# Neighbourhood attention with tokens ordered by grid columns: blocks of 64 queries over 128 keys

## The reference

```python
col = jnp.arange(GRID_W)                       # GRID_W = 64
col_start = jnp.clip(col - NA_COLS // 2, 0, GRID_W - NA_COLS)      # NA_COLS = 16
col_mask = (col[None, :] >= col_start[:, None]) & (col[None, :] < col_start[:, None] + NA_COLS)
...
sc = jnp.einsum('bhqd,bhrkd->bhqrk', qi, kr).astype(jnp.float32)
sc = sc + jnp.transpose(bias, (0, 2, 1, 3))[None]
sc = jnp.where(col_mask[:, None, :], sc, NEG_INF)
p = jax.nn.softmax(sc.reshape(b, N_HEADS, GRID_W, kh * GRID_W), axis=-1).reshape(sc.shape)
return jnp.einsum('bhqrk,bhrkd->bhqd', p.astype(vr.dtype), vr)
```

## Time and profile before

| | us |
|---|---|
| median of 3 runs | 1767.66 (1767.57 to 1767.67) |
| the profiled execution, its own time | 1768.03 |
| its span in the trace | 1766.1 |
| PE busy | 1757.5 |
| DVE busy | 1232.5 |
| ACT busy | 994.0 |
| POOL busy | 97.8 |

### The profile page before, as it was taken

One profiled execution on the slowest core, in us unless ns is written; L12 is line 12 of the kernel. 1 busy time (PEld: TensorE's weight loads), 2 busy tenths in 40 slices (PEclk: granted clock), 3 DMA queues, 4 the chain that ended last, 5 costly groups with the idle time before them and its releaser, 6 DMA issues.

```text
span 1766.1 us, 25241 instructions
## 1 busy us (share of the span) xinstructions
PE 1757.5 (100%) x9960; PEld 1503.2 (85%) x9960; DVE 1232.5 (70%) x1897; ACT 994.0 (56%) x1580; POOL 97.8 (6%) x179
## 2 busy tenths in 40 slices
PE   8999999999999999999999999999999999999999
PEld 7878888888888888888888888888888888888887
DVE  5877774668776677567755887776487648778763
ACT  6666553555555655456545666554565446656551
POOL 0000000511110000000001110000000001100000
PEclk9999999999999999999999999999999999999999
DMA  9335565453343455545563344555365534336552
GB/s 354 133 145 189 191 227 191 178 189 144 144 155 144 168 191 203 214 150 187 190 215 132 132 167 162 200 189 214 138 218 191 214 122 168 144 143 215 191 212 75
DMA packets 45080, 314.72 MB, mean 178 GB/s; under 512 B 5008, under 2 KB 5520, under 8 KB 7968
## 3 DMA queue, kind: packets, MB, share of 16 engines
q1 hardware_dynamic: 44640, 312.54, 48.8%
q10 hardware_dynamic: 288, 0.52, 0.1%
q0 software_dynamic: 32, 0.03, 0.0%
HBM read 312.03 MB, written 1.05 MB: 177 GB/s over the span
## 4 chain that ended last, share of the span: by engine, by line
PE 99%; DMA 0%; DVE 0%; ACT 0%; SPq 0%; issue 0%
PE P L404 96%; PE P L699 1%; PE P L411 1%; DMA raw<-w_all 0%; ACT xx L1239 0%; PE P L1117 0%; PE P L1037 0%; PE P L605 0%; DVE xx L1790 0%; PE P L983 0%; DVE xs L1810 0%; PE P L1060 0%; PE P L931 0%; ACT wh L1217 0%; PE P L921 0%
## 5 line engine op out<-in xcount | busy, mean ns | idle before, releaser
L1755 DVE TENSOR_TENSOR wl<-raw,wh 128x2048 fp32r<-128x2048 f32 x287 | 656.9, 2295 | 190.4 <-ACT wh L1211 171.3
L1211 ACT ACTIVATE wh<-raw 128x2048 fp32r<-128x2048 f32 x291 | 551.8, 1900 | 194.5 <-PE P L404 170.4
L404 PE MATMUL P<-xx,wh 128*128 128x512 f32 (+2 forms) x2800 | 652.1, 385 | 0.0
L404 PEld LDWEIGHTS P<-xx,wh 128*128 128x128 f32 (+1 forms) x2800 | 503.0, 188 | 100.1 <-issue 4.3
L404 PEld LDWEIGHTS P<-xx,wl 128*128 128x128 f32 x2688 | 344.4, 191 | 12.4
L404 PE MATMUL P<-xx,wl 128*128 128x256 f32 x2688 | 350.7, 283 | 0.0
L1340 ACT ACTIVATE ft<-P 128x256 f32<-128x256 f32 x240 | 90.3, 383 | 230.7 <-PE P L404 230.7
L404 PE MATMUL P<-wh,fhh 128*128 128x512 f32 x528 | 206.2, 390 | 0.0
L404 PE MATMUL P<-wh,fhl 128*128 128x512 f32 x528 | 205.5, 389 | 0.0
L404 PE MATMUL P<-wl,fhh 128*128 128x512 f32 x528 | 205.5, 389 | 0.0
L1916 DVE TENSOR_TENSOR fg<-P,ft 128x256 f32<-128x256 f32 x240 | 101.8, 424 | 121.7 <-ACT ft L1340 116.5
(11 more groups left out here) (323 smaller groups left out, 1485.5 us busy)
## 6 DMA issues: line engine op xcount, KB each, us to landing
raw<-w_all SPq DMA_DIRECT2D x289, 1024.0 KB, 4.8
nB<-rpb SPq DMA_DIRECT2D x4, 768.0 KB, 8.8
raw<-w_all SPq DMA_DIRECT2D x2, 512.0 KB, 7.3
fgb<-post SPq DMA_DIRECT2D x2, 512.0 KB, 5.5
out<-xs SPq DMA_DIRECT2D x4, 256.0 KB, 2.0
C<-cst SPq DMA_DIRECT2D x1, 769.0 KB, 7.9
xs<-x_in ACTq DMA_DIRECT2D x2, 256.0 KB, 3.9
xs<-x_in SPq DMA_DIRECT2D x1, 512.0 KB, 7.4
```

What stands on the lines that cost most here:

```text
L404: return t_.on.matmul(o, l, r, start=start, stop=stop, skip_group_check=True)
L1211: a.on.activation(o, i, ACT.Copy).then_inc(*hi.up((m,)))
L1755: v.on.tensor_tensor(o, i, h.bitcast(F32), ALU.subtract).then_inc(*lo.up(m))
```

## The change

The tokens of the attention step are ordered by grid column, number = 4 * column + row, while the rest of the kernel keeps the old order. A block of 64 queries (16 columns) then needs at most 32 columns, which are 128 neighbouring keys. Keys are kept at their number modulo 128, so that a tile of scores is 128 queries by 128 places.

- x is loaded in the new order into `nx` (the buffer `ntm`), and a second time in the old order into `xs`, after piece 10, for the residual sum.
- `scores_na` makes four blocks of 64 queries. `SEGMENTS` lists for each the pieces of keys (first key, place, width), six in all, and each is one matmul a head.
- Bias, maximum, exponential and scaling work on two times 128 columns a head instead of two times 256. The bias is 2 MB instead of 3 MB.
- Two transposes a head instead of four.
- `nV` has four parts: the values of the 128 keys of each block. ACT writes parts 0 and 3, and POOL builds parts 1 and 2 from them in twelve copies of 512 columns, six for each half of the heads. `values_na` makes one sum over 128 keys for each of four blocks of 64 queries.
- The output copies read PSUM in the order of columns and write in the old order (`natural`, `columns`).

```diff
+SEGMENTS = [[(0, 0, 128)], [(32, 32, 96), (128, 0, 32)], [(128, 0, 96), (96, 96, 32)], [(128, 0, 128)]]
...
+        def placed(t, d):
+
+            return x_in[0, :, d].rearrange("(r c) d -> c r d", r=4)[32 * t:32 * t + 32, :, :]
+
+        def natural(ap):
+            return ap.rearrange("p (r c) -> p r c", r=4)
+
+        def columns(ap):
+            return ap.rearrange("p (c r) -> p r c", r=4)
...
-            q.on.dma_start(xs[:, 1, :], x_in[0, toks(1), :]).then_inc(*s_x[1][0].up(0))
+            q.on.dma_start(nx[:, 1, :], placed(1, slice(0, D))).then_inc(*s_x[1][0].up(0))
...
+                if m == RAW + 7:
+                    q.on.dma_start(xs[:, :, :], x_in[0].rearrange("(t p) d -> p t d", t=2)).then_inc(*s_res.up(0))
...
-                for t in range(2):
-                    for h in range(2):
-                        q = AN["nq"][64 * h:64 * h + 64, p % 4, :]
-                        k = mul(P[2 + h][:, t * S:(t + 1) * S], q[:, toks(t)], q[:, S:2 * S], True, True)
+                for b in range(4):
+                    o = 64 * (b % 2)
+                    for key, at, w in SEGMENTS[b]:
+                        for h in range(2):
+                            q = AN["nq"][64 * h:64 * h + 64, p % 4, :]
+                            at_ = b // 2 * 128 + at
+                            k = mul(P[2 + h][o:o + 64, at_:at_ + w], q[:, 64 * b:64 * b + 64], q[:, S + key:S + key + w],
+                                    True, True)
...
-                t_.wait_ge(*aa.of("V", 0, 3))
-                for y in range(2):
+                t_.wait_ge(*aa.of("V", 0, p // 4))
+                t_.wait_ge(*aa.of("V", 0, 2 + p // 4))
+                t_.wait_ge(*ga.of("V", p // 4, 5))
+                for y in range(4):
                     for h in range(2):
                         t_.wait_ge(*aa.of("c", 0, p, h))
-                        k = mul(P[b][64 * h:64 * h + 64, 0:S], AN["nV"][:, y, (2 * p + h) * 64:(2 * p + h) * 64 + 64],
-                                NTA[h][:, y * S:(y + 1) * S], y == 0, y == 1)
+                        k = mul(P[b][64 * h:64 * h + 64, 64 * y:64 * y + 64],
+                                AN["nV"][:, y, (2 * p + h) * 64:(2 * p + h) * 64 + 64], NTA[h][:, 64 * y:64 * y + 64], True, True)
...
-                probs(0, p, NPA, (4, 5) if p < 7 else (2, 3), (0, 2, 1, 3))
+                probs(0, p, NPA, (4, 5) if p < 7 else (2, 3), (0, 1))
...
-                a.on.activation(AN["noh"][:, p, :], P[obank(p)][:, 0:S], ACT.Copy).then_inc(*ax.up(("oh", 0, p)))
+                a.on.activation(natural(AN["noh"][:, p, :]), columns(P[obank(p)][:, 0:S]), ACT.Copy).then_inc(*ax.up(("oh", 0, p)))
...
-                both_scores(0, p, NPA, AN["nsmA"], ((0, 256), (256, 256)), bias, 1.0)
+                both_scores(0, p, NPA, AN["nsmA"], ((0, 128), (128, 128)), bias, 1.0)
...
+                if s == 0:
+                    v.wait_ge(*s_res.of(0))
...
+            for hf in range(2):
+                g.wait_ge(*aa.of("V", 0, hf))
+                g.wait_ge(*aa.of("V", 0, 2 + hf))
+                if hf:
+                    g.wait_ge(*ga.of("V", 0, 5))
+                V_ = AN["nV"][:, :, halfs(hf)]
+                for i, (y, p0, p1, src) in enumerate(((1, 0, 32, 3), (1, 32, 64, 0), (1, 64, 128, 0), (2, 0, 64, 3), (2, 64, 96, 3),
+                                                      (2, 96, 128, 0))):
+                    if i:
+                        g.wait_ge(*ga.of("V", hf, i - 1))
+                    g.on.tensor_copy(V_[p0:p1, y, :], V_[p0:p1, src, :]).then_inc(*ga.up(("V", hf, i)))
```

More of the change, by code:

```diff
@@ L410, in turn @@
                 for j in range(4):
-                    k = t_.on.transpose(P[b][:, toks(j)], xs[:, t, (4 * q + j) * 128:(4 * q + j + 1) * 128], ident)
+                    k = t_.on.transpose(P[b][:, toks(j)], (xs if s else nx)[:, t, (4 * q + j) * 128:(4 * q + j + 1) * 128], ident)
                 k.then_inc(*tx.up(("turn", s, t, q)))
@@ L1243, in squares @@
                 a.wait_ge(*(s_x[t][h * (1 - t)].of(0) if s == 0 else vx.of("x", s - 1, h, t)))
-                a.on.activation(SQJ[s][:, t, halfs(h)], xs[:, t, halfs(h)], ACT.Square, bias=0.0, scale=1.0,
+                a.on.activation(SQJ[s][:, t, halfs(h)], (xs if s else nx)[:, t, halfs(h)], ACT.Square, bias=0.0, scale=1.0,
                                 accum_out=ss[:, 2 * h + t:2 * h + t + 1]).then_inc(*ax.up(("sq", s, h, t)))
@@ L1428, in probs_na @@
             def probs_na(p):
-                both_probs(0, p, NTA, (4, 5) if p < 7 else (2, 3))
+                both_probs(0, p, NTA, (4, 5) if p < 7 else (2, 3), 256)
             def exps_na(p):
-                exps(0, p, NPA, AN["nsmA"], ((0, 256), (256, 256)), 1.0)
+                exps(0, p, NPA, AN["nsmA"], ((0, 128), (128, 128)), 1.0)
             def probs_dil(n):
@@ L1460, in na @@
                 for i in range(4):
-                    a.on.activation(AN["nV"][:, i // 2, halfs(i % 2)], P[2 + i][:, :], ACT.Identity, bias=0.0,
+                    a.on.activation(AN["nV"][:, i // 2 * 3, halfs(i % 2)], P[2 + i][:, :], ACT.Identity, bias=0.0,
                                     scale=rr_[:, i // 2:i // 2 + 1]).then_inc(*aa.up(("V", 0, i)))
@@ L2017, in bias @@
                 def bias(h, z):
-                    at = (2 * p + h) * 384 + 128 - 128 * z
-                    return AN["nB"][:, at:at + 256]
-                both_scores(0, p, NPA, AN["nsmA"], ((0, 256), (256, 256)), bias, 1.0)
+                    at = (2 * p + h) * 256 + 128 * z
+                    return AN["nB"][:, at:at + 128]
+                both_scores(0, p, NPA, AN["nsmA"], ((0, 128), (128, 128)), bias, 1.0)
             def shares_na(p):
-                shares(0, p, NPA, AN["nsmA"], ((0, 256), (256, 256)))
+                shares(0, p, NPA, AN["nsmA"], ((0, 128), (128, 128)))
             def scores_dil(n):
@@ L2035, in out_na @@
                 v.wait_ge(*ax.of("oh", 0, p))
-                v.on.tensor_tensor(AN["nol"][:, p, :], P[obank(p)][:, 0:S], AN["noh"][:, p, :].bitcast(F32),
-                                   ALU.subtract).then_inc(*vx.up(("ol", 0, p)))
+                v.on.tensor_tensor(natural(AN["nol"][:, p, :]), columns(P[obank(p)][:, 0:S]),
+                                   natural(AN["noh"][:, p, :].bitcast(F32)), ALU.subtract).then_inc(*vx.up(("ol", 0, p)))
             def out_dil(f):
@@ L2669, in packed @@
             put(name, l, np.tile(inputs[name][l], (128, 1)))
-    rpb = np.full((2, 64, NH, 6, 64), NEG, np.float32)
-    for i in range(2):
-        for q in range(64):
-            a = min(max(q - 8, 0), 48)
-            b = a + 16
-            rpb[i, q, :, :, a:b] = inputs["na_rpb"][0][:, 5 - i:11 - i, a - q + 15:b - q + 15]
-    rpb = rpb.reshape(128, NH * 384)
+    rpb = np.full((128, NH, 2, 128), NEG, np.float32)
+    for n in range(256):
+        q, i = divmod(n, 4)
+        a = min(max(q - 8, 0), 48)
+        for k in range(4 * a, 4 * a + 64):
+            rpb[n % 128, :, n // 128, k % 128] = inputs["na_rpb"][0][:, k % 4 - i + 7, k // 4 - q + 15]
+    rpb = rpb.reshape(128, NH * 256)
     post = np.stack([inputs["norm_mix_post"][0], inputs["norm_ffn_post"][0], inputs["norm_mix_post"][1],
```

14 lines of the change are left out of this document (8 added, 6 removed).

## The result

| | before | changed |
|---|---|---|
| median, us | 1767.66 (1767.57 to 1768.0, 4 runs) | 1757.05 (1756.9 to 1757.1, 4 runs) |
| the profiled execution, its own time | 1768.03 | 1757.08 |
| its span | 1766.1 | 1755.3 |

The ratio is 0.9939, with a 95% interval from 0.9922 to 0.9957: the changed kernel is 10.6 us faster, where 9.0 were forecast: 1757.05 us lies under the 1757.8 to 1760.2 that the prediction gave to its own case A. The whole interval lies beyond the 0.2% that a measurement tells from no change.

The account below looks back on a forecast made before the run. TensorE was taken to bound the kernel. Transposes 3.5, sums of values 3.2 and scores 2.4 us gave 9.1, called 9.0: from 1768.03 to 1759.0, or 1758.7 us as a median; its own range was 1757.8 to 1760.2.

Parts of the forecast that it names:

- case A: The prediction's own case, all terms summed: 1758.7 us, range 1757.8 to 1760.2, chance 0.60.
- What bounds: TensorE bounds the attention section, so a microsecond of its work removed there is a microsecond off the end.
- Transposes, 3.5 us: TensorE's attention transposes: four fewer a pair at 0.11 us each, 3.5 us saved over eight pairs.
- Sums of values, 3.2 us: TensorE's sums of values: eight matmuls of 64 columns replace four of 256, 0.61 us instead of 1.01, saving 3.2 us.
- Scores, 2.4 us: TensorE's attention scores: twelve small matmuls started in program order, a group of 0.75 us instead of 1.07, saving 2.4 us.
- Rival B: Scores: array halves run freely and 32-column passes are cheap, saving 3.8 us; time 1757.3 us, chance 0.15.
- The start, 0: Program start: the read of x by grid column was counted as nothing, at most 0.5 us of lateness.
- What must stay hidden: Attention period: DVE at 7.4 us and ACT at 6.0 fit in 7.6; POOL's copies and DMA stay hidden too.
- The lateness at pair 1's scores: TensorE asks DVE earlier at pair 1's scores: about 0.3 us wait without gain from halved widths, none with; counted nothing.
- rival D: Every attention period: TensorE asks DVE too early and waits 0.3 to 0.6 us; time about 1762.5, chance 0.05.
- Rival E: Pair 0's sum of values waits for slow POOL copies, making the kernel slower: 1774.4 us, chance 0.03.
- Rival C: Scores: blocks do not overlap, a group of 1.15 us, losing 0.6 us; time 1761.7; chance 0.15 together with unsaved sums.

Follow-up runs that it names:

- e8: The changed kernel with four transposes a head instead of two, the extra two unused; 1760.63 us, ratio 0.9961 to the kernel before.
- e5: The changed kernel with keys of score blocks 1 and 2 in pieces of 64 and 64 instead of 96 and 32; 1757.34 us.
- e3: The changed kernel with its score blocks issued in the order 0, 2, 1, 3 instead of 0, 1, 2, 3; 1759.68 us.
- e9: The changed kernel again, unaltered, x read by columns; 1758.71 us (1757.19 to 1759.02), ratio 0.9946 to the kernel before.
- e7: The changed kernel with sums of values of the old size, two steps over 256 columns; 1760.67 us, ratio 0.9961 to the kernel before.
- e12: The changed kernel with one 128-key piece a score block, POOL's second-half copies held until q and k of pair 3 are made; 1757.04 us.
- e6: The changed kernel with one 128-key piece a score block and sixteen POOL copies instead of twelve; 1758.21 us.

## Why the prediction was right or wrong

**What bounds.** Right. TensorE was busy in all of the old period and is in all of the new one. Every microsecond taken from its three groups came off the span; the three runs with one part undone show it for each part.

**Transposes, 3.5 us.** Right: 0.529 us a group against 0.53 forecast, 3.5 us, and e8 gives them back.

**Sums of values, 3.2 us.** Right: 0.615 us against 0.61. The rule of the Trainium skill ("TensorE: Matmul & The Clock Gate", Part 3) that a weight load overlaps a running matmul only in another row group would, by the prediction's estimate, have made this group 1.03 us; it is 0.615, with 64-column passes over all 128 rows. Here the trace disagrees with it.

**Scores, 2.4 us.** This is the step that failed, and in its mechanism: the overlap. "If issue is in order" and "block 3 cannot pass them: 382 + 218 = 600, a group of 0.75 us" were the words. Block 3 does pass them: it starts before block 2's second pass of 96 and before its 32 columns. The group is 0.661 us and saves 3.2 us, 0.8 more than forecast. Had block 3 waited for the first pass of the 32 columns, it would have started 0.118 us later by the records, and the group would be about 0.78 us (an estimate: 0.661 + 0.118), near the 0.75 forecast; so the order alone accounts for this error. The 0.058 us for 32 columns was too dear (e5) but has no part in it, since block 3's start at 382 and the 600 don't contain it. Rival B, with free halves and cheap 32s, had 0.59 us and a saving of 3.8; the measured 3.2 lies between it and the case taken. The 0.65 us that the prediction worked out for free halves with dear 32s comes nearest, but by luck: the 32s are not so dear, block 3's first pass takes 0.139 us where the second of block 0, as wide, takes 0.109, and the halves are not free of each other's order (e3). The argument in the prediction, that the 64x64 rows show "a start in program order", went too far: in rows of equal matmuls nothing has an occasion to pass, so they can't tell.

**The start, 0.** "I take nothing, and at most 0.5 us" had a loss in mind. It is a gain of 0.9 us in the changed kernel's profile. Between spans of the same kernel with x by columns and by rows it is 0.4 to 0.8 us for the changed kernel (1755.27 and 1755.44 against 1756.03 and 1755.81) and 0.3 for the one before (1765.86 against 1766.12 and 1766.15). Of the 0.9, the changed kernel with x by rows keeps 0.1 and 0.3 (its product with `rr` starts at 32.89 and 32.72 against 33.00), little more than two executions of one kernel differ by there (0.17 between these, 0.10 between those of the kernel before). I had asked only when x itself lands, and not what else becomes earlier when x comes later. In the profiles the mechanism is shown; its size in the medians is not.

With these two, 9.0 + 0.8 + 0.9 = 10.7, against the 10.6 measured and the 10.8 of the spans. That the sum meets the median so closely is in part luck: e9, the same kernel, has a median of 1758.71, the forecast to 0.01 us, though its groups are those of the changed kernel, and its fastest run 1757.19. The groups' lengths, alike in all eight pairs, decide what was right here, and not the median of one measurement.

**What must stay hidden.** Right. DVE needs 6.42 us of 7.50 and ACT 5.04 (7.4 and 6.0 were the bounds without credit for the halved widths, and the halving gave the rest). The output copies were priced by those of the dilated attention, 0.63 and 0.62 us; the reordered ones take no longer than before, which the tiles view shows (against the earlier trace rows):

```profile
L1426 ACT ACTIVATE noh<-P x8: 377/378/404, 59.4 to 103.9; 128x256 fp32r<-128x256 f32 x8
```

```profile
L2059 DVE TENSOR_TENSOR nol<-P,noh x8: 417/418/426, 61.1 to 104.3; 128x256 fp32r<-128x256 f32 x8
```

The lateness at pair 1's scores, which I bounded by 0.3 us and counted as nothing, is real but small. By the starts it is 0.35 us over pairs 1 and 2 in e5, 0.28 and 0.26 in pair 2 of e7 and e9, 0.12 and 0.13 in e12 and e6, and none in the changed kernel's first profile. So rival D (a wait in every period) fell, and its mechanism exists at the start: the three profiles with the most have a weight split of 2.66 to 2.73 us beside POOL's copies, the changed kernel's first one of 2.36. (e3 has 2.67 and no wait; its longer score groups let PE ask later.) POOL's copies, timeline and tiles view:

```profile
34.84 10.68 POOL L2582 COPY nV<-nV 32x512 f32<-32x512 f32 x12 [12.22 <-ACT nV L1482]
```

```profile
L2582 POOL COPY nV<-nV x12: 607/616/2560, 34.8 to 44.9; 32x512 f32<-32x512 f32 x8, 64x512 f32<-64x512 f32 x4
```

All twelve are done at 45.5, and the first sum of values starts at 55.42. A copy takes 0.61 us, and up to 2.56 beside one of DVE's weight splits, where I had taken 1.4 and at most 2.87. Rival E was 10 us away, and that with all twelve and not only the first six. Rival C (blocks that don't overlap, 1.15 us) fell with the first profile.

## What to carry to other kernels

Where one engine is busy all the time, price a group of small matmuls by rows of like shapes in the same trace; two of three such terms were right to 0.1 us over eight pairs. A view of equal instructions can't tell whether they would pass each other if they were unequal: where the order decides a term, keep both ends or price it by the pass count alone. When a transfer at the start is made slower to issue, ask also which other transfers then land earlier, and who waits for those. And when the busiest engine starts earlier, see from the distance of its instructions at which clock they ran: what e3 won by an earlier start it lost by a later rise of the clock.

## What the hardware showed that I had not expected

- Small fp32 matmuls for the two column halves of the array start out of program order: a score group of 0.661 us with blocks 0, 1, 2, 3 and of 0.929 us with 0, 2, 1, 3, the same matmuls in both.
- Two matmuls of 96 and 32 columns cost hardly more than two of 64 (0.661 against 0.648 us a group), and one of 128 is cheaper than either (0.598).
- A read of x in strided order takes 0.62 us to issue instead of 0.40 to 0.46. Its packets start 0.1 to 0.3 us later, and that is enough for a small transfer issued beside it to get through first: the identity lands at 2.5 to 3.3 us instead of 3.8 to 4.0.
- TensorE's clock rose from its lower level to the full one at 6.27 us in one profile of the changed kernel, at 7.67 in the other, and at 12.25 in e3, whose program is the same up to there. Weight matmuls ahead of it start 0.427 us apart and not 0.231, while the row by window says 1.00.
- POOL's copies and DVE's weight split wait for each other. In the changed kernel a copy that starts inside the split takes 2.56 us instead of 0.61 and ends 0.48 us after it. A split that starts while a copy runs is longer: 2.29 us where the copy has 0.00 us left (e6), 2.36 where it has 0.22 (changed kernel), 2.66 with 0.52 (e9), 2.73 with 0.58 (e5). In the changed kernel's timeline of DVE the split that was running when the first copy started, and the one that started during a copy, are:

```profile
33.00 2.29 DVE L1776 TENSOR_TENSOR wl<-raw,wh 128x2048 fp32r<-128x2048 f32 x1 [1.41 <-ACT wh L1232]
...
40.54 2.36 DVE L1776 TENSOR_TENSOR wl<-raw,wh 128x2048 fp32r<-128x2048 f32 x1 [0.92 <-ACT wh L1232]
```
